# Scan of the second block: running sums loaded by DMA, and the per-head work put into another order

## The chip, the core and the metric

The kernel runs on one core of a Trainium2 chip. The time is the device time of the program in microseconds; the median of three runs counts. Five engines work from their own queues, in order: TensorE (PE, matrix products), VectorE (DVE), ScalarE (ACT, functions by table), GpSimd (POOL) and SyncE (SP), which here issues every DMA. They meet only in semaphore waits.

## The reference

Two transformer blocks on one sequence of 512 positions with 1024 channels, all in float32. The change touches only the scan in the mixer of the second block:

```python
a_cum = jnp.cumsum(log_a, axis=-1)
seg = a_cum[..., :, None] - a_cum[..., None, :]
decay_in = jnp.exp(jnp.where(causal, seg, -jnp.inf))
cb = jnp.einsum("bclgn,bcsgn->bcgls", cc, bc)
y_diag = jnp.einsum("bcgjls,bcsgjp->bclgjp", cb[:, :, :, None] * decay_in, x_)
decay_to_end = jnp.exp(a_cum[..., -1:] - a_cum)
states = jnp.einsum("bclgn,bcgjl,bclgjp->bcgjpn", bc, decay_to_end, x_)
...
y_off = jnp.einsum("bclgn,bcgjpn,bcgjl->bclgjp", cc, prev, jnp.exp(a_cum))
```

There are 32 heads in 4 groups of 8, and 4 chunks of 128 positions. `log_a` is `dt * a`, a number for each position and head; `a_cum` is its running sum inside a chunk.

## The kernel before

**Weights.** All weight products are cut into 361 units of 8 blocks. A block is one 128x128 piece of a weight times 128x512 of the input, in three matmuls (L755, L757, L759), since each float32 operand is split into a high part and a remainder. For each unit SP loads 512 KB into one of three raw buffers (L1892), ACT rounds it to the high part (L1128, a "cut") and DVE subtracts (L1420, the second half of the cut). The cut is ticked three units before its use.

**Order.** `score()` writes one list of ticks by hand. Each engine walks through the whole list and issues what it has for each tick, so the list sets the order on every engine. `woven(main, side, every, lead)` lets `lead` blocks of the main work pass and then puts one step of the side work behind every `every` blocks. In `seg(g)` (g = 1 to 4) the main work is 64 to 112 blocks and the side work is `ssd(g - 1)`, the scan of one group. Segment 1 runs `ya_main` beside group 0; segments 2, 3 and 4 begin with `zgroup(g - 2)`, four tiles z of 8 blocks each. The ticks of two finished z tiles are held and released together, behind blocks 16 and 32. A z tile costs ACT a silu (L1263), DVE a product (L1580), ACT a square (L1145) and, for the second and third of a group, POOL an addition (L1842). There is one buffer for the silu, so the steps of two tiles follow one another across ACT and DVE.

**The scan of a group.** `xrow` (four times) turns x on PE (L1030) and DVE scales it by dt into XD (L1739). `bturn` turns B (PE L1038, ACT L1370). `cb` is C times B (PE L1046), masked by DVE (L1746). `state` c = 0, 1, 2: POOL scales XD[c] by the decay to the chunk's end into the one buffer `stmp` (L1866), PE multiplies (L1054), DVE carries the sum on (L1752; L1756 and L1758). `decay` of a head: PE spreads the head's row of running sums to all 128 partitions by a product of a column of `pairR` with `acR`, the sums in high part and remainder (L1063); ACT makes `exp` of three chunks into EX (L1378), the differences by four Relu (L1381) and their `exp` into SGM (L1384); DVE multiplies SGM by CB (L1764) and POOL multiplies EX by C (L1872). SGM and EX have six buffers for eight heads, so heads 6 and 7 wait for the output of heads 0 and 1. `output` j: PE makes the result of heads 2j and 2j + 1 (L1073, L1079), which needs their SGM and EX and all three states; DVE adds the skip term (L1770).

**Tables.** ACT's Exp and Silu lie in different function tables; between them stands an ACT_TABLE_LOAD.

Below, "turn" always means one of the four xrow steps, and block k of a segment is counted from the segment's start; the first turn of each group stands behind block 6.

## Time and profile before

| | us |
|---|---|
| runs | 2361.22, 2362.50, 2362.77 |
| median | 2362.5 |
| profiled execution, its own time | 2362.4 |
| span of its profile | 2360.6 |
| PE busy (share of the span) | 2302.7 (98%) |
| DVE, ACT, POOL busy | 1168.1, 870.8, 155.1 |
| group 0 of the scan, first turn to about the last output | 1433 to 1475 |
| groups 1, 2 and 3 | 1529 to 1577, 1612 to 1660, 1695 to 1742 |

The span is what the profile's clock covers; the execution's own time is 1.8 us more. The stretches are times from the span's start. PE is the engine that sets the end, so the question for any work on another engine is whether PE waits for it.

### The profile page before, as it was taken

Reading aid. Unit: us, or ns where it says so; the run is one execution under the profiler, and the core shown is the slowest. Engines: PE = TensorE matmul, PEld = TensorE weight load, DVE = VectorE, ACT = ScalarE, POOL = GpSimd, SP = SyncE. Lnnn points to the kernel's source line nnn. Section 1 sums busy time; section 2 is a strip of 40 time slices with the busy share of each in tenths; the row PEclk is TensorE's granted clock in tenths of the full one; section 3 lists DMA queues with packets and bytes.
Section 4 is the critical chain, followed back from the end, with each engine's and each line's share of the span. In section 5 each row is a group of like instructions: output and inputs, shape, how many; then the busy total and the mean of one; then the engine's idle time right before and its main releaser. Section 6 shows DMA issues by size and latency. Waiting matters only on the chain.

```text
span 2360.6 us, 27446 instructions
## 1 busy us (share of the span) xinstructions
PE 2302.7 (98%) x11216; PEld 1842.1 (78%) x11216; DVE 1168.1 (49%) x1615; ACT 870.8 (37%) x1413; POOL 155.1 (7%) x145
## 2 busy tenths in 40 slices
PE   8999999999999999999999999999999999999998
PEld 6767788888777677888887877866778887888886
DVE  3765665543465744333335455556743345553453
ACT  3554322132354533322323236356363223332332
POOL 1111000000100010000010002022020001000001
PEclk9999999999999999999999999999999999999999
DMA  9323465522212122222232222211223222233222
GB/s 318 134 99 111 175 216 202 207 98 98 81 63 72 46 71 83 96 98 98 90 107 81 98 90 98 98 55 63 72 90 107 98 81 98 87 101 106 92 88 81
DMA packets 77518, 250.69 MB, mean 106 GB/s; under 512 B 8272, under 2 KB 16720, under 8 KB 77392
## 3 DMA queue, kind: packets, MB, share of 16 engines
q1 hardware_dynamic: 77392, 248.93, 30.4%
q8 instruction: 89, 1.46, 0.3%
q14 instruction: 37, 0.30, 0.0%
HBM read 244.70 MB, written 4.19 MB: 105 GB/s over the span
## 4 chain that ended last, share of the span: by engine, by line
PE 82%; ACT 3%; DVE 3%; issue 1%; POOL 1%; POOLq 0%; DVEq 0%; ACTq 0%
PE pb L755 25%; PE pb L759 24%; PE pb L757 24%; PE pb L979 1%; PE pb L1004 1%; PE pb L989 1%; PE pb L1073 1%; DVE slab L1684 1%; PE pb L779 1%; PE pb L775 1%; PE pb L777 1%; PE pb L1054 1%; PE pb L800 0%; PE pb L861 0%; ACT slab L1381 0%
## 5 line engine op out<-in xcount | busy, mean ns | idle before, releaser
L755 PE MATMUL pb<-hhi,whi 128*128 128x512 f32 x1976 | 787.0, 398 | 4.2 <-ACT hhi L1156 2.4
L1420 DVE TENSOR_TENSOR wlo<-raw,whi 128x1024 fp32r<-128x1024 f32 x361 | 449.1, 1248 | 686.9 <-ACT whi L1128 686.9
L757 PE MATMUL pb<-hhi,wlo 128*128 128x512 f32 x1976 | 771.3, 390 | 1.7 <-DVE wlo L1420 1.7
L759 PE MATMUL pb<-hlo,whi 128*128 128x512 f32 x1976 | 771.4, 390 | 0.4 <-DVE hlo L1416 0.4
L1128 ACT ACTIVATE whi<-raw 128x1024 fp32r<-128x1024 f32 x361 | 379.2, 1056 | 688.8 <-PE pb L759 672.0
L755 PEld LDWEIGHTS pb<-hhi,whi 128*128 128x128 f32 x1976 | 371.2, 188 | 98.5 <-issue 24.5
L759 PEld LDWEIGHTS pb<-hlo,whi 128*128 128x128 f32 x1976 | 371.2, 188 | 81.8 <-DVE hlo L1416 1.6
L757 PEld LDWEIGHTS pb<-hhi,wlo 128*128 128x128 f32 x1976 | 371.7, 188 | 78.8 <-DVE wlo L1420 2.7
L755 PE MATMUL pb<-ahi,whi 128*128 128x512 f32 x848 | 336.2, 396 | 1.4 <-ACT ahi L1310 0.7
L759 PE MATMUL pb<-alo,whi 128*128 128x512 f32 x848 | 331.3, 391 | 0.0
L757 PE MATMUL pb<-ahi,wlo 128*128 128x512 f32 x848 | 331.2, 391 | 0.0
L755 PEld LDWEIGHTS pb<-ahi,whi 128*128 128x128 f32 x848 | 159.9, 189 | 39.2 <-issue 6.1
L759 PEld LDWEIGHTS pb<-alo,whi 128*128 128x128 f32 x848 | 159.7, 188 | 34.5 <-DVE alo L1416 0.8
L757 PEld LDWEIGHTS pb<-ahi,wlo 128*128 128x128 f32 x848 | 159.9, 189 | 32.7 <-issue 0.7
L1842 POOL TENSOR_TENSOR slab<-slab 128x512 f32<-128x512 f32 x44 | 62.0, 1410 | 1588.2 <-ACT slab L1145 1587.3
L1511 DVE SCALAR_TENSOR_TENSOR slab<-slab,vec 128x509 f32<-128x509 f32 (+2 forms) x132 | 99.0, 750 | 4.7
L1416 DVE TENSOR_TENSOR alo<-slab,ahi 128x512 fp32r<-128x512 f32 x90 | 62.3, 692 | 67.9 <-ACT ahi L1227 50.4
L1431 DVE SCALAR_TENSOR_TENSOR slab<-slab,small 128x1024 f32<-128x1024 f32 x70 | 89.9, 1284 | 1.9
L1145 ACT ACTIVATE slab<-X 128x512 f32<-128x512 f32 x48 | 30.3, 632 | 109.3 <-PE pb L759 39.5
L1684 DVE TENSOR_TENSOR_SCAN slab<-slab,cst 128x128 f32<-128x128 f32 (+3 forms) x64 | 52.5, 820 | 31.0 <-ACT slab L1323 31.0
L1542 DVE TENSOR_TENSOR slab<-slab,pb 128x512 f32<-128x512 f32 x66 | 45.0, 682 | 43.6 <-PE pb L759 43.6
L1227 ACT ACTIVATE ahi<-slab 128x512 fp32r<-128x512 f32 x66 | 41.7, 632 | 66.0 <-DVE slab L1542 65.8
(232 smaller groups left out, 1702.9 us busy)
## 6 DMA issues: line engine op xcount, KB each, us to landing
raw<-stream SPq DMA_DIRECT2D x361, 512.0 KB, 3.3
slab<-ada_w SPq DMA_DIRECT2D x80, 512.0 KB, 5.0
early<-ada_w SPq DMA_DIRECT2D x32, 256.0 KB, 7.6
X<-xT SPq DMA_DIRECT2D x8, 256.0 KB, 4.5
ya<-slab SPq DMA_DIRECT2D x8, 256.0 KB, 2.3
slab<-ya SPq DMA_DIRECT2D x8, 256.0 KB, 4.9
outT<-X SPq DMA_DIRECT2D x8, 256.0 KB, 2.1
cst<-consts SPq DMA_DIRECT2D x1, 576.0 KB, 7.2
```

The source lines that it names most:

```text
L755: e.matmul(out, wh, hi, start=s.k == 0, stop=False)
L757: e.matmul(out, wl, hi, start=False, stop=False)
L759: i = e.matmul(out, wh, lo, start=False, stop=s.last)
L1128: e.activation(whi[:, u % NW, :], raw[:, u % NRAW, :], ACT.Copy).then_inc(*a_cut.up(u))
L1227: e.activation(a_out[f % HALF][0], SG[f % 6], ACT.Copy).then_inc(*a_half.up(("f", l, f)))
L1416: e.tensor_tensor(out, src, hi.bitcast(F), ALU.subtract).then_inc(*v_half.up(key))
L1420: e.tensor_tensor(wlo[:, u % NW, :], raw[:, u % NRAW, :], whi[:, u % NW, :].bitcast(F), ALU.subtract).then_inc(*v_cut.up(u))
L1431: e.scalar_tensor_tensor(o, a, cond[:, k:k + 1], o, ALU.mult, ALU.add).then_inc(*v_mod.up(("fma", n)))
L1511: e.scalar_tensor_tensor(t[:, d:], u[:, :S - d], W(name, (width - 1 - d) * tiles + i), t[:, d:], ALU.mult, ALU.add).then_inc(*v_conv.up((k ...
L1542: e.tensor_tensor(t, t, b, ALU.mult).then_inc(*v_ev.up(tile))
L1684: e.tensor_tensor_scan(p[:, 0:wd][:, ::-1], RS[n % 4][:, 0:wd][:, ::-1], C("late", S - wd)[:, 0:wd][:, ::-1], 1.0, ALU.mult, ALU.max).then ...
L1842: e.tensor_tensor(acc, acc, sq_of(sid, d), ALU.add).then_inc(*p_sum.up((sid, d)))
```

## The change

- `decay` has no PE part any more. DVE's sums `dtac` are written to DRAM once (`sums_dram`, 32 heads by 512 positions), and SP loads the row of each head into EX on all 128 partitions, in head order, two heads ahead of the decay that reads it; the load of head n waits for the output of head n - 6. `acR`, `pairR`, and the ACT and DVE steps that filled them are gone.
- ACT's part of `decay` reads EX (in SBUF) instead of the PSUM bank, first the four Relu, then the `exp` of three chunks in place, then the other.
- DVE's and POOL's part of `decay` is now a tick of its own, `masked`.
- `ssd` has another order: decays 0 and 1 stand between the turns, decay 2 at bturn, and so on; one step behind every 2 blocks for all groups (before: 2 for group 0, 1.2 for the others), but 17 steps instead of 25.
- POOL scales XD[0] and XD[1] at their turns into two buffers `STMP`, and XD[2] at the tick of state 0.

```diff
-SSD_FIRST, SSD_NEXT = 2, 1.2
+SSD_EVERY = 2
...
     def ssd(g):
         for c in range(4):
             tick("xrow", g, c)
+            if c % 2 == 0:
+                tick("decay", g, c // 2)
             yield 1
         tick("bturn", g)
+        tick("decay", g, 2)
         yield 1
         tick("cb", g)
+        tick("masked", g, 0)
         yield 1
-        for c in range(3):
-            tick("state", g, c)
-            yield 1
-        for j in range(4 + SKEW):
-            if j < 4:
-                for hh in (2 * j, 2 * j + 1):
-                    tick("decay", g, hh)
-                    yield 1
-            if j >= SKEW:
-                tick("output", g, j - SKEW)
-                yield 2
+        tick("state", g, 0)
+        tick("decay", g, 3)
+        tick("masked", g, 1)
+        yield 1
+        tick("state", g, 1)
+        tick("masked", g, 2)
+        yield 1
+        tick("state", g, 2)
+        tick("decay", g, 4)
+        tick("masked", g, 3)
+        yield 1
+        tick("decay", g, 5)
+        for j in range(4):
+            tick("output", g, j)
+            if j < 2:
+                tick("decay", g, 6 + j)
+                tick("masked", g, 4 + j)
+            if j in (1, 2):
+                tick("masked", g, 5 + j)
+            yield 2
...
-            e.matmul(b, pairR[:, H:H + 1].to_broadcast([64, P]), acR[:, :], start=True, stop=True).then_inc(*t_ssd.up(("decay", g, h)))
...
-            e.activation(ex[:, P:], b[:, P:], ACT.Exp).then_inc(*a_ssd.up(("ex", g, h)))
-                m = e.activation(sg[:, quarter(c)], b[:, quarter(c)], ACT.Relu, bias=nat[:, o:o + 1], scale=-1.0)
+                m = e.activation(sg[:, quarter(c)], ex[:, quarter(c)], ACT.Relu, bias=nat[:, o:o + 1], scale=-1.0)
             m.then_inc(*a_ssd.up(("fall", g, h)))
             w.wait_ge(a_ssd, ("fall", g, h))
+            e.activation(ex[:, P:], ex[:, P:], ACT.Exp).then_inc(*a_ssd.up(("ex", g, h)))
...
+        def scaled_rows(g, c):
...
+            if c == 2:
+                w.wait_ge(t_ssd, ("state", g, 0))
             elif g:
+                w.wait_ge(t_ssd, ("state", g - 1, 2))
...
+        def fall():
+
+            n = falls[0]
+            if n < 32:
+                falls[0] += 1
+                if n >= 6:
+                    w.wait_ge(t_ssd, ("y", *divmod(n - 6, 8)))
+                e.dma_start(EX[n % 6], sums_dram[n:n + 1, :].to_broadcast([P, S])).then_inc(*d_ac[n % 6].up(n))
```

Where the steps now stand. **ACT, group 1, from its last cut ahead of the group.** L1263 and L1145 are silu and square of the z tiles, L1370 is the turned B. Before, the two z tiles stand ahead of all heads:

```order
L1370 ACTIVATE spare_67<-pb 128x512
L1263 ACTIVATE slab<-pb 128x512
L1145 ACTIVATE slab<-slab 128x512
L1263 ACTIVATE slab<-pb 128x512
L1145 ACTIVATE slab<-slab 128x512
L1128 ACTIVATE whi<-raw 128x1024
L1378 ACT_TABLE_LOAD
L1378 ACTIVATE slab<-pb 128x384
L1381 ACTIVATE slab<-pb,slab 128x128 x4
L1384 ACTIVATE slab<-slab 128x512
```

Now (L1373 is the turned B; L1383, L1386, L1387 are the Relu and the two exp of a head; L1268 and L1150 silu and square):

```order
L1387 ACTIVATE slab<-slab 128x512
L1133 ACTIVATE whi<-raw 128x1024
L1383 ACTIVATE spare_68<-spare_71,slab 128x128 x4
L1386 ACTIVATE spare_71<-spare_71 128x384
L1387 ACTIVATE spare_68<-spare_68 128x512
L1373 ACTIVATE spare_66<-pb 128x512
L1383 ACTIVATE spare_69<-spare_72,slab 128x128 x4
L1386 ACTIVATE spare_72<-spare_72 128x384
L1387 ACTIVATE spare_69<-spare_69 128x512
L1268 ACT_TABLE_LOAD
L1268 ACTIVATE slab<-pb 128x512
L1150 ACTIVATE slab<-slab 128x512
```

Three heads have moved ahead of the z tiles, and what stands behind the tiles begins with a cut and a table load again; ACT_TABLE_LOAD stands 28 times in the program, before 22.

**DVE, group 1, from the turns to the third head.** L1739 is XD, L1746 CB, L1752, L1756 and L1758 the states, L1580 the product of a z tile, L1764 the product with CB. Before:

```order
L1739 TENSOR_TENSOR slab<-pb,slab 128x512 x2
L1746 TENSOR_TENSOR slab<-pb,cst 128x512
L1752 COPY slab<-pb 128x512
L1756 TENSOR_TENSOR slab<-slab 128x512
L1758 TENSOR_TENSOR slab<-slab,pb 128x512
L1756 TENSOR_TENSOR slab<-slab 128x512
L1758 TENSOR_TENSOR slab<-slab,pb 128x512
L1580 TENSOR_TENSOR slab<-slab 128x512 x2
L1420 TENSOR_TENSOR wlo<-raw,whi 128x1024
L1764 TENSOR_TENSOR slab<-slab 128x512
```

Now (L1583 is the z product, L1423 the cut):

```order
L1739 TENSOR_TENSOR slab<-pb,slab 128x512 x3
L1583 TENSOR_TENSOR slab<-slab 128x512 x2
L1423 TENSOR_TENSOR wlo<-raw,whi 128x1024
L1746 TENSOR_TENSOR slab<-pb,cst 128x512
L1764 TENSOR_TENSOR slab<-slab 128x512
L1752 COPY slab<-pb 128x512
L1764 TENSOR_TENSOR spare_68<-spare_68,slab 128x512
L1756 TENSOR_TENSOR slab<-slab 128x512
L1758 TENSOR_TENSOR slab<-slab,pb 128x512
L1764 TENSOR_TENSOR spare_69<-spare_69,slab 128x512
```

The z products and the cut have moved ahead of CB and of every state, and products of heads stand between the states.

**POOL, group 1.** L1866 scales XD, L1842 is the addition for the z tiles, L1872 (now L1880) the product of a head. Before:

```order
L1866 TENSOR_TENSOR spare_68<-slab 128x512 x3
L1842 TENSOR_TENSOR slab<-slab 128x512
L1872 TENSOR_TENSOR slab<-slab 128x384
L1872 TENSOR_TENSOR spare_72<-spare_72,slab 128x384
L1872 TENSOR_TENSOR spare_73<-spare_73,slab 128x384
```

Now:

```order
L1866 TENSOR_TENSOR spare_67<-slab 128x512
L1866 TENSOR_TENSOR stmp_60<-slab 128x512
L1842 TENSOR_TENSOR slab<-slab 128x512
L1880 TENSOR_TENSOR slab<-slab 128x384
L1866 TENSOR_TENSOR spare_67<-slab 128x512
L1880 TENSOR_TENSOR spare_71<-spare_71,slab 128x384
L1880 TENSOR_TENSOR spare_72<-spare_72,slab 128x384
```

The third scaling has moved behind the addition and behind a head's product.

**DVE, group 1, at the last outputs.** L1770 is the skip term of an output. Now the last head's product stands behind two z products and a cut:

```order
L1770 SCALAR_TENSOR_TENSOR slab<-slab,vec,pb 128x512
L1764 TENSOR_TENSOR slab<-slab 128x512 x2
L1583 TENSOR_TENSOR slab<-slab 128x512 x2
L1423 TENSOR_TENSOR wlo<-raw,whi 128x1024
L1770 SCALAR_TENSOR_TENSOR slab<-slab,vec,pb 128x512
L1764 TENSOR_TENSOR spare_68<-spare_68,slab 128x512
L1770 SCALAR_TENSOR_TENSOR slab<-slab,vec,pb 128x512
```

Before, it stood ahead of them:

```order
L1764 TENSOR_TENSOR slab<-slab 128x512
L1764 TENSOR_TENSOR spare_69<-spare_69,slab 128x512
L1770 SCALAR_TENSOR_TENSOR slab<-slab,vec,pb 128x512 x2
L1580 TENSOR_TENSOR slab<-slab 128x512 x2
L1420 TENSOR_TENSOR wlo<-raw,whi 128x1024
L1770 SCALAR_TENSOR_TENSOR slab<-slab,vec,pb 128x512
```

## Rows read from the trace of the kernel before

**Rows 1.** PE waits in the four groups, microseconds 1400 to 1800: total, times, longest.

```profile
PE pb L1054 <- POOL spare L1866: 5.4, 7, 1.1
PE pb L1073 <- DVE spare L1764: 3.8, 2, 1.9
PE pb L1073 <- DVE slab L1764: 2.1, 2, 1.9
```

**Rows 2.** Timeline of PE around one head's spreading product: start, duration, engine, line.

```profile
1452.01 0.40 PE L759 MATMUL pb<-alo,whi 128*128 128x512 f32 x1
1452.33 0.49 PE L1063 MATMUL pb<-acR,pairR 64*128 64x512 f32 x1
...
1453.09 0.40 PE L757 MATMUL pb<-ahi,wlo 128*128 128x512 f32 x1
1453.33 0.39 PE L759 MATMUL pb<-alo,whi 128*128 128x512 f32 x1
```

**Rows 3.** Windows of groups 1 and 2: length, busy (count) PE, PEld, DVE, ACT, POOL, clock, DMA.

```profile
1529.40:1577.00 47.60, 43.94 (x259) 30.66 (x257) 24.87 (x31) 29.38 (x65) 15.61 (x13) 0.96 0.14 45
1612.20:1660.00 47.80, 44.19 (x260) 31.17 (x258) 25.93 (x33) 29.64 (x65) 15.61 (x13) 0.96 0.15 52
```

**Rows 4.** Timeline of PE, group 0: first turn, states 0 and 1.

```profile
1433.34 0.60 PE L1030 MATMUL pb<-cst,slab 128*128 128x128 f32 x4
...
1444.75 1.02 PE L1054 MATMUL pb<-spare,spare 128*128 128x512 f32 x2
...
1447.11 1.10 PE L1054 MATMUL pb<-spare,spare 128*128 128x512 f32 x2
```

**Rows 5.** Timeline of PE, group 1: first turn, last state, outputs.

```profile
1529.41 0.60 PE L1030 MATMUL pb<-cst,slab 128*128 128x128 f32 x4
...
1542.59 1.10 PE L1054 MATMUL pb<-spare,spare 128*128 128x512 f32 x2 [1.08 <-POOL spare L1866]
...
1555.67 0.29 PE L1073 MATMUL pb<-slab 128*64 128x128 f32 x1 [1.95 <-DVE spare L1764]
...
1563.11 0.66 PE L1073 MATMUL pb<-spare,slab 128*64 128x128 f32 x8
...
1567.05 0.66 PE L1073 MATMUL pb<-slab 128*64 128x128 f32 x8
```

**Rows 6.** Timeline of ACT, group 1: cut, z tiles, cut, table, heads.

```profile
1529.66 1.04 ACT L1128 ACTIVATE whi<-raw 128x1024 fp32r<-128x1024 f32 x1
...
1545.78 0.63 ACT L1145 ACTIVATE slab<-slab 128x512 f32<-128x512 f32 x1 [10.12 <-DVE slab L1580]
...
1547.65 0.63 ACT L1145 ACTIVATE slab<-slab 128x512 f32<-128x512 f32 x1 [0.76 <-DVE slab L1580]
1548.19 1.04 ACT L1128 ACTIVATE whi<-raw 128x1024 fp32r<-128x1024 f32 x1
1549.25 1.28 ACT L1378 ACT_TABLE_LOAD   x1
...
1552.63 0.47 ACT L1378 ACTIVATE spare<-pb 128x384 f32<-128x384 f32 x1
```

**Rows 7.** Timeline of DVE, group 1: state 2's two steps, then a z product.

```profile
1543.73 0.69 DVE L1756 TENSOR_TENSOR slab<-slab 128x512 f32<-128x512 f32 x1 [1.46 <-PE pb L1054]
...
1545.06 0.68 DVE L1580 TENSOR_TENSOR slab<-slab 128x512 f32<-128x512 f32 x1
```

**Rows 8.** Timeline of POOL, group 1: third scaling, z addition.

```profile
1540.97 1.48 POOL L1866 TENSOR_TENSOR spare<-slab 128x512 f32<-128x512 f32 x1 [1.39 <-PE pb L1054]
1548.42 1.28 POOL L1842 TENSOR_TENSOR slab<-slab 128x512 f32<-128x512 f32 x1 [5.98 <-ACT slab L1145]
```

**Rows 9.** DMA issues: KB each, median us from issue to landing.

```profile
ya<-slab SPq DMA_DIRECT2D x8, 256.0 KB, 2.3
slab<-ya SPq DMA_DIRECT2D x8, 256.0 KB, 4.9
```

**Rows 10.** Timeline of ACT ahead of group 2: the last silu before it.

```profile
1613.43 0.72 ACT L1364 ACTIVATE slab<-slab,vec 128x512 f32<-128x512 f32 x1 [3.12 <-DVE slab L1511]
```

More of the change, by code:

```diff
@@ L478, in score @@
     for g in range(1, 5):
[L479 removed]
+        run(woven(seg(g), ssd(g - 1), SSD_EVERY, SSD_LEAD))
     run(woven(zgroup(3), gated(2), 8))
@@ L555, in program @@
     d_late = signal("d_late", 16)
+    d_ac = [signal(f"d_ac{i}", 16) for i in range(6)]
+    d_sums = signal("d_sums", 16)
     d_ya = [signal(f"d_ya{i}", 16) for i in range(KD)]
@@ L1053, in state @@
             w.wait_ge(p_ssd, ("st", g, c))
-            e.matmul(b, Bn[:, quarter(c)], stmp, start=True, stop=True).then_inc(*t_ssd.up(("state", g, c)))
+            e.matmul(b, Bn[:, quarter(c)], STMP[c % 2], start=True, stop=True).then_inc(*t_ssd.up(("state", g, c)))
             give(("state", g, c), v_ssd, ("state", g, c))
-        def decay(g, h):
-            H = 8 * g + h
-            b = take(("decay", g, h))
-            w.wait_ge(a_ssd, "achi")
-            w.wait_ge(v_ssd, "aclo")
-            w.wait_ge(v_ssd, "pair")
-            e.matmul(b, pairR[:, H:H + 1].to_broadcast([64, P]), acR[:, :], start=True, stop=True).then_inc(*t_ssd.up(("decay", g, h)))
-            give(("decay", g, h), a_ssd, ("fall", g, h))
         def output(g, j):
@@ L1087, in tensor @@
               "values": values, "start": start, "turn": turn, "gather": gather, "dtturn": dtturn, "xrow": xrow, "bturn": bturn,
-              "cb": cb, "state": state, "decay": decay, "output": output}
+              "cb": cb, "state": state, "output": output}
         for name, *a in ticks:
@@ L1911, in evac, with dtturn @@
                 e.dma_start(ya_dram[i], SPILL[i % 4]).then_inc(*d_ya[i].up("out"))
+        def dtturn():
+            w.wait_ge(v_ssd, ("scan", 3))
+            e.dma_start(sums_dram, dtac[0:32, :]).then_inc(*d_sums.up("out"))
+            w.wait_ge(d_sums, "out")
+            for _ in range(2):
+                fall()
+        falls = [0]
+        def fall():
[5 more added lines that the diff above has]
+                e.dma_start(EX[n % 6], sums_dram[n:n + 1, :].to_broadcast([P, S])).then_inc(*d_ac[n % 6].up(n))
         def fetch(i):
@@ L1939, in sync @@
         fma(16)
-        do = {"cut": lambda u: load() if u > 2 else None, "fma": fma, "evac": evac, "fetch": fetch, "final": final}
+        do = {"cut": lambda u: load() if u > 2 else None, "fma": fma, "evac": evac, "dtturn": dtturn, "decay": lambda g, h: fall(), "fetch": fetch, "final": final}
         for name, *a in ticks:
```

39 lines of the change are left out of this document (17 added, 22 removed).

## The prediction

> **What bounds the kernel now.** The page's table comes first: TensorE is busy for 98% of the span, so the end moves only by what TensorE no longer has to do or no longer waits for. The second view is the list of waits between microseconds 1400 and 1800, where the four groups of the scan lie [rows 1]: TensorE waits 5.4 us for GpSimd's scaled rows (L1866) ahead of the states, and 3.8 and 2.1 us for VectorE's products with CB (L1764) ahead of an output. The third is TensorE's timeline, which gives the price of one inserted step, and the windows of two groups for its clock. The fourth is the timelines of ScalarE, VectorE and GpSimd in group 1, because the new order has to be walked through on each of their queues.
>
> **The change part by part.**
>
> *The spreading products go.* From the L759 ahead of one to the second matmul behind it pass 1453.09 - 1452.01 = 1.08 us; two matmuls without it are 2 x 0.23 [rows 2]. One costs 0.62 us of TensorE's path, and 32 of them 19.8 us. Nothing hides it: this is the sure part.
>
> *The old waits.* They are 11.3 us [rows 1]. Behind the longest, the clock was granted at 0.96 of full speed in groups 1 and 2 [rows 3]: up to 0.04 x 47.6 = 1.9 us of work lost each, of which part fell into the idle time; I take 1.2 us each, 2.4 us. So the old order costs 19.8 + 11.3 + 2.4 = 33.5 us above a TensorE that never waits. The question is what the new order costs above the same line.
>
> *The grid of the new order.* It puts a step behind every second block, as group 0 had it. First turn to state 0 is 1444.75 - 1433.34 = 11.41 us, a state with two blocks about 2.27 us (1447.11 less 0.09 idle) [rows 4]. An output with three blocks takes 1567.05 - 1563.11 = 3.94 us [rows 5], with four 4.63. In group 1 the first turn is at 1529.41 [rows 5], so without waits state 0 stands at 1540.8, state 2 at 1545.4, output 0 at 1547.6 (its end at 1549.4), and output 3 at 1561.5.
>
> *ScalarE in group 1.* Its last cut begins at 1529.66, so head 0 begins at 1530.7. A table load takes 1.28 us; a head took 1552.63 - 1549.25 - 1.28 = 2.1 us from PSUM [rows 6]. Reading SBUF instead is not in the trace for this step; I bound it by 0 and 0.25 us (0.05 for each of five instructions, the spread between this engine's pitches) and take 2.13. Two z tiles cost a table load and two rounds of 1547.65 - 1545.78 = 1.87 us, 5.1 with the handovers, as long as VectorE answers at once; a cut takes 1.0 [rows 6]. In the new queue: head 0 to 1534.1, cut 1535.1, head 1 1537.2, turned B 1537.9, head 2 1540.0, z tiles 1545.1, cut 1546.2, head 3 with its table load 1549.5, head 4 1551.6.
>
> *VectorE.* The new queue has the z products and the cut ahead of CB and of the states. The cut waits for ScalarE's 1546.2 and ends at 1547.4. Then come CB, head 0, state 0, head 1, at 0.6 us each (two steps, of which one waits for the other, take 1545.06 - 1543.73 = 1.33 [rows 7]): head 1 is done at 1549.9. State 1, head 2 and state 2 end at 1553.2. Output 0 could start at 1547.6, and needs state 2 for its last quarter: it ends at 1553.7, 4.3 us late. So the wait for CB products doesn't go; it is handed on to a queue that now waits for the cut.
>
> *GpSimd.* The scalings 0 and 1 are early, and cost TensorE nothing any more. Scaling 2 stands behind the addition for the z tiles, which waits for ScalarE's second square at 1545.1. The addition takes 1.28 us, a head's product I bound by the same, the scaling took 1.48 [rows 8]: 1549.0 to 1549.2. State 2 is 3.7 us late, mostly inside the same delay, since output 0 waits for VectorE anyway; with half a microsecond of slower clock output 0 ends at 1554.2.
>
> *The loads.* 32 loads of 256 KB ride in SP's queue. Heads 0 to 5 of a group find theirs landed two heads ahead. Heads 6 and 7 can't: their buffer is free when output 0 ends. Landing is not in the trace for a repeated row; the bounds are 2.3 and 4.9 us of two other 256 KB transfers [rows 9], and I take 2.3, since nothing else is queued there. Behind the waiting SP stand the loads of the weight stream, issued three units (16 us) ahead of use, which a wait of 3 us doesn't exhaust. Behind the waiting ScalarE stand the z tiles and a cut. So head 6 starts at 1554.2 + 0.1 + 2.3 = 1556.6, heads 6 and 7 end at 1560.9, the z tiles at 1566.1, the cut at 1567.1, VectorE's half of it at 1568.4, the skip term of output 2 and the product of head 7 at 1569.7. Output 3 waits for this one: 1569.7 - 1561.5 = 8.2 us late in group 1.
>
> *Groups 2 and 3* begin with ScalarE later. The last silu ahead of group 2 is at 1613.43 [rows 10]; carried back by the distance of the groups (83.0 us) that is 1530.5 against about 1529.0, hence 1.4 us later all along, and 0.4 more where the cut behind block 24 now waits for a late TensorE. 10.0 us late each. *Group 0* has no z tiles: walked in the same way, ScalarE ends head 7 at about 1460 and output 3 is due at 1465. No wait, about 0.3 us of handovers.
>
> *Clock.* Each of the three groups gets a stall of over 3 us ahead of output 3. One such stall cost 1.2 us in two groups and nothing in the third; 0.8 each, 2.4 us, between 0 and 5.7 (three times the 1.9 above).
>
> *Table loads.* Six more on ScalarE. The order of groups 1 to 3 above contains them; where they hide nothing else changes. In the trace a load takes 1.28 us and the next instruction starts at once [rows 6]. The Trainium skill, "ScalarE: Activation LUTs", section "What ACT_TABLE_LOAD costs", gives 2.66 us a switch, with 1.38 of draining behind the load. By that the chains of three groups would each be some 4 us longer, and the kernel about 2371. This case's rows show no such drain, and they decide.
>
> *Nothing else.* ScalarE's and VectorE's one-time steps for the old operands go, under cover of TensorE's blocks; the write of the sums and its wait stand 30 us ahead of the first head.
>
> **The sum.** New order: 0.3 + 8.2 + 10.0 + 10.0 + 2.4 = 30.9 us, old order 33.5. The profiled execution took 2362.4 us, 0.1 below the median. 2362.5 - 2.6 is 2359.9; as VectorE's and ScalarE's steps in the walk are rounded up to their handovers, I take 0.5 us less: 2359.4. The products leave TensorE, and nearly all of it comes back as waits, because ScalarE is now the limit inside a group: 8 heads, 4 z tiles, 3 cuts and 4 table loads are 17 + 7.5 + 3 + 5.1 = 33 us of unbroken work between head 0 and the last cut, and the grid leaves 31 us for it.
>
> **The rivals.**
> - *Full gain.* The heads begin early enough that TensorE never waits. For it speaks that ScalarE idled 10.12 us at the z tiles before [rows 6], which the new order lets it use. Against it stand the 33 us. It would give 2362.5 - 33.5 + 0.3 = 2329.
> - *ScalarE's work alone.* If the buffers of heads 6 and 7 were filled without delay behind output 0, output 3 would be 1.9 us less late in group 1, and 2.3 in the others; about 2353.
> - *Late loads, slower than before.* A row of DRAM read 128 times lands late. ScalarE waits for it at head 6, in front of the z tiles and the cut, and TensorE pays each microsecond three times. At 4.9 us [rows 9] it is 3 x 2.6 = 7.8 us more: 2367. With the clock at its upper bound 2370. It decides from a landing of 3.4 us for slower at all, 5 us (or 4 with the clock) for slower than can be told.
>
> **How the numbers follow.** Forecast 0.54, full gain 0.10, ScalarE alone 0.14, late loads 0.22. About 0.2% (4.7 us) is what a measurement can tell from no change. The forecast's own range is 2355 to 2364 (heads at 2.1 or 2.35 us, clock 0 to 5.7); of its 0.54, 0.18 is faster than 2357.8 and 0.36 inside. Late loads are 0.18 slower and 0.04 inside. Faster 0.42, same 0.40, slower 0.18. The range leaves out the full gain and part of the rest: 2350 to 2369.
>
> **What would show it.** Right: no L1063, 32 loads into EX; TensorE waits at output 3 of groups 1 to 3 for L1764, 3 to 5 us each, at state 2 for L1866, 3 to 4 us, and not at all in group 0; ScalarE without idle time from head 0 on except at head 6. Wrong: a TensorE without these waits (the full gain), or loads that land in over 3.4 us. My walk through the queues would be wrong if VectorE came to CB before the cut was ready.

## The result, and the profile after

The changed kernel takes 2378.3 us (median of 6 runs, 2375.5 to 2379.8); the kernel before, on the same chip, 2361.5 us (median of 6). The ratio is 1.0071, with a 95% interval of 1.0060 to 1.0082: slower, by about 17 us. The forecast was 2359.4 with a range to 2369.0, so the time lies outside it and on the other side. The profiled execution took 2376.0 us, with a span of 2373.9 us (2360.6 before).

The list of PE's waits in the four groups, microseconds 1430 to 1790 (what is waited for: us in total, times, longest), answers to [rows 1]. L1068 is the state's matmul, L1078 and L1084 are an output's, L1866 is GpSimd's scaling, L1764 VectorE's product with CB:

```profile
PE pb L1068 <- POOL spare L1866: 17.3, 3, 6.2
PE pb L1078 <- DVE spare L1764: 11.2, 2, 5.7
PE pb L1078 <- DVE slab L1764: 7.4, 2, 5.5
PE pb L771 <- DVE wlo L1423: 1.4, 2, 0.7
PE pb L1084 <- DVE slab L1758: 1.1, 1, 1.1
```

The 11.3 us of before have become 37.0 (the L771 row, a wait for a cut, is left out: before has 1.7 us of the same). They stand where the prediction put them: state 2 and output 3 of groups 1 to 3. PE's timeline of group 1 shows both, and what follows the first one (L769, L771 and L773 are the three matmuls of a block):

```profile
1547.23 2.04 PE L1068 MATMUL pb<-spare,spare 128*128 128x512 f32 x2 [4.84 <-POOL spare L1866]
1548.29 1.42 PE L769 MATMUL pb<-hhi,whi 128*128 128x512 f32 x1
1549.50 0.63 PE L771 MATMUL pb<-hhi,wlo 128*128 128x512 f32 x1
1549.93 0.63 PE L773 MATMUL pb<-hlo,whi 128*128 128x512 f32 x1
...
1550.65 0.40 PE L771 MATMUL pb<-hhi,wlo 128*128 128x512 f32 x1
1550.88 0.40 PE L773 MATMUL pb<-hlo,whi 128*128 128x512 f32 x1
...
1571.05 0.44 PE L1078 MATMUL pb<-slab 128*64 128x128 f32 x1 [5.73 <-DVE spare L1764]
```

The state's matmul takes 2.04 us where it took 1.02 [rows 4], and the next products follow one another at 0.43 us, then at 0.23. The windows say why (columns as in [rows 3]; the clock is third from the end):

```profile
1526.00:1573.00 47.00, 36.43 (x230) 27.97 (x230) 25.84 (x30) 33.69 (x67) 17.36 (x13) 0.91 0.31 101
1612.00:1660.00 48.00, 36.29 (x223) 27.71 (x223) 27.93 (x33) 33.82 (x67) 17.10 (x13) 0.89 0.32 107
...
1571.00:1574.00 3.00, 2.96 (x28) 2.88 (x28) 0.00 (x0) 0.00 (x0) 0.00 (x0) 0.50 0.44 164
```

The granted clock of the two groups is 0.91 and 0.89, against 0.96 before, and behind output 3 it is 0.50: TensorE works at 1.2 GHz instead of 2.4, after 5.7 us without work.

In some executions of every kernel, before too, the scan begins some 5 us earlier than in others (first turn of group 0 at 1428.5 instead of 1433.3), since TensorE's clock stays up at places far ahead of it; so intervals inside the scan are compared first, and medians second.

**An account that every run below uses.** Take the interval from group 1's first turn to group 2's. Subtract TensorE's idle time (the bracketed waits of its timeline, without those of 0.2 us), then the work lost to the lower clock (over windows of 1 us, busy time times one less the granted clock), then what the kernel adds to TensorE's queue: 8 spreading products, or filler. The rest should be the same in all kernels. It is read from one profiled execution of each.

| kernel | interval | idle | lower clock | products or filler | rest |
|---|---|---|---|---|---|
| before | 82.95 | 4.4 | 1.7 | 5.0 | 71.9 |
| after | 86.35 | 11.3 | 3.2 | 0 | 71.9 |
| d1 new order, products | 87.56 | 8.4 | 3.4 | 4.4 | 71.4 |
| d2 old order, loads | 84.83 | 10.5 | 2.3 | 0 | 72.0 |
| d3 no late loads | 82.28 | 8.7 | 1.4 | 0 | 72.2 |
| d4 third buffer | 86.68 | 9.1 | 5.8 | 0 | 71.8 |
| e5 slower pace | 77.52 | 4.5 | 2.3 | 0 | 70.7 |
| e8 filler | 85.06 | 2.1 | 0 | 11.2 | 71.8 |
| f4 filler, state 2 only | 86.32 | 8.6 | 1.4 | 4.3 | 72.0 |
| h1 head 5 early | 73.32 | 1.8 | 0 | 0 | 71.5 |
| h2 the same, products | 76.66 | 0.7 | 0 | 4.4 | 71.6 |

The rests lie between 70.7 and 72.2 us. Over all four groups the changed kernel idles 25.8 us more than before (2.7, 6.9, 8.1 and 8.1), loses 12.1 us instead of 3.3 to the lower clock (6.1 behind state 2 and 6.1 behind output 3), and saves 19.8 us of products: 14.8 us slower. Measured from the first turn of group 0 to the last group norm's spreading product are 12.5 us (-3.0, +3.4, +5.3 and +6.9 in the four groups). Another 0.9 us comes behind it, where the changed kernel's execution lost 1.6 us to the lower clock and that of before none.

Three more views. GpSimd in group 1: the addition, a head's product and the scaling that state 2 waits for:

```profile
1542.43 1.27 POOL L1842 TENSOR_TENSOR slab<-slab 128x512 f32<-128x512 f32 x1 [7.35 <-ACT slab L1150]
1543.66 1.98 POOL L1880 TENSOR_TENSOR slab<-slab 128x384 f32<-128x384 f32 x1
1545.60 1.49 POOL L1866 TENSOR_TENSOR spare<-slab 128x512 f32<-128x512 f32 x1
```

ScalarE in group 1: a table load and what follows it; head 6, which waits for its load:

```profile
1537.13 1.28 ACT L1268 ACT_TABLE_LOAD   x1
1538.42 0.60 ACT L1268 ACTIVATE slab<-pb 128x512 f32<-128x512 f32 x1
...
1556.91 1.28 ACT L1383 ACTIVATE slab<-slab 128x128 f32<-128x128 f32 x4 [2.28 <-DMA slab<-sums]
```

And the DMA issues (KB each, median us from issue to landing), which answer to [rows 9]:

```profile
raw<-stream SPq DMA_DIRECT2D x361, 512.0 KB, 3.4
slab<-sums SPq DMA_DIRECT2D x17, 256.0 KB, 3.7
spare<-sums SPq DMA_DIRECT2D x15, 256.0 KB, 3.8
```

### The profile page after: what moved, and what is told of

It is laid out like the page before. It is cut to its first block, busy times and chain, and to the rows that moved or that the text cites. A ratio compares the mean times of both kernels' runs of the same rounds, so it can differ in the third digit from the quotient of the medians.

```text
span 2373.9 us, 27414 instructions
## 1 busy us (share of the span) xinstructions
PE 2291.4 (97%) x11184; PEld 1846.1 (78%) x11184; DVE 1176.3 (50%) x1613; ACT 883.9 (37%) x1418; POOL 158.4 (7%) x145
## 4 chain that ended last, share of the span: by engine, by line
PE 78%; DVE 5%; ACT 4%; issue 2%; DMA 1%; POOL 0%; DVEq 0%; POOLq 0%; SPq 0%; ACTq 0%
PE pb L769 24%; PE pb L773 23%; PE pb L771 23%; DVE slab L1514 1%; PE pb L993 1%; PE pb L1018 1%; DVE wlo L1423 1%; PE pb L1003 1%; ACT whi L1133 1%; ACT slab L1383 1%; DVE slab L1687 1%; PE pb L793 1%; PE pb L789 1%; PE pb L791 1%; PE pb L814 0%
## 5 line engine op out<-in xcount | busy, mean ns | idle before, releaser
L1423 DVE TENSOR_TENSOR wlo<-raw,whi 128x1024 fp32r<-128x1024 f32 x361 | 448.3, 1246 | 708.8 <-ACT whi L1133 708.8
L769 PE MATMUL pb<-hhi,whi 128*128 128x512 f32 x1976 | 786.8, 398 | 3.4 <-ACT hhi L1161 2.2
L771 PE MATMUL pb<-hhi,wlo 128*128 128x512 f32 x1976 | 772.1, 391 | 1.4 <-DVE wlo L1423 1.4
L773 PE MATMUL pb<-hlo,whi 128*128 128x512 f32 x1976 | 772.4, 391 | 0.4 <-DVE hlo L1419 0.4
L769 PEld LDWEIGHTS pb<-hhi,whi 128*128 128x128 f32 x1976 | 372.3, 188 | 94.8 <-issue 20.1
L773 PEld LDWEIGHTS pb<-hlo,whi 128*128 128x128 f32 x1976 | 371.8, 188 | 82.3 <-DVE hlo L1419 1.6
L771 PEld LDWEIGHTS pb<-hhi,wlo 128*128 128x128 f32 x1976 | 372.3, 188 | 80.4 <-issue 3.2
L769 PE MATMUL pb<-ahi,whi 128*128 128x512 f32 x848 | 335.5, 396 | 1.4 <-ACT ahi L1315 0.7
L773 PE MATMUL pb<-alo,whi 128*128 128x512 f32 x848 | 331.0, 390 | 0.0
L771 PE MATMUL pb<-ahi,wlo 128*128 128x512 f32 x848 | 331.0, 390 | 0.0
L769 PEld LDWEIGHTS pb<-ahi,whi 128*128 128x128 f32 x848 | 159.9, 189 | 37.3 <-issue 4.2
L773 PEld LDWEIGHTS pb<-alo,whi 128*128 128x128 f32 x848 | 159.7, 188 | 34.2 <-DVE alo L1419 0.7
L771 PEld LDWEIGHTS pb<-ahi,wlo 128*128 128x128 f32 x848 | 160.1, 189 | 33.1 <-issue 0.7
L1842 POOL TENSOR_TENSOR slab<-slab 128x512 f32<-128x512 f32 x44 | 61.8, 1405 | 1596.8 <-ACT slab L1150 1595.9
L1150 ACT ACTIVATE slab<-X 128x512 f32<-128x512 f32 x48 | 30.3, 632 | 109.2 <-PE pb L773 39.5
```

The lines of the kernel that those rows point to most:

```text
L769: e.matmul(out, wh, hi, start=s.k == 0, stop=False)
L771: e.matmul(out, wl, hi, start=False, stop=False)
L773: i = e.matmul(out, wh, lo, start=False, stop=s.last)
L1423: e.tensor_tensor(wlo[:, u % NW, :], raw[:, u % NRAW, :], whi[:, u % NW, :].bitcast(F), ALU.subtract).then_inc(*v_cut.up(u))
L1842: e.tensor_tensor(acc, acc, sq_of(sid, d), ALU.add).then_inc(*p_sum.up((sid, d)))
```

## The experiments

Each median stands beside that of the kernel before from the same chip.

**1. Order alone, loads alone.** The first kernel is the changed one with the old products on TensorE; the second is the old order with the loads.

```diff
 d1, against after
-    e.dma_start(EX[n % 6], sums_dram[n:n + 1, :].to_broadcast([P, S]))
+    e.matmul(b, pairR[:, H:H + 1].to_broadcast([64, P]), acR[:, :], ...)
 d2, against before
-    e.matmul(b, pairR[:, H:H + 1].to_broadcast([64, P]), acR[:, :], ...)
+    e.dma_start(EX[n % 6], sums_dram[n:n + 1, :].to_broadcast([P, S]))
```

> The kernel before with only the new order of the scan (heads between the turns, the products with CB ticked on their own, two buffers for the scaled rows); the running sums still come from the spreading product on TensorE. The order theory: what makes the changed kernel slow is the order, since the z tiles now stand ahead of CB, of the states and of the third scaling, and ahead of head 7's product. Then the waits at state 2 and output 3 of groups 1 to 3 are here too. The 32 products (0.62 us each) come back, but 24 of them fall into those waits, and the landing time ahead of head 6 (2.3 us of idle ScalarE) goes: about 2378, between 2374 and 2381. The load theory: the slow part is the loads (landing 3.7 us, SyncE held up to 8 us in front of the weight loads, 8 MB more traffic); without them the new order is as good as it looks, and the time is 2366 or less.

> The changed kernel with the old order of the scan (all heads behind the states, steps 2 and 1.2 blocks apart, one buffer for the scaled rows, filled at each state), but with the running sums loaded. The order theory: the products leave TensorE (19.8 us less work), and the old waits grow, because head 1 is bound by ScalarE's queue and TensorE now arrives at output 0 some 3.7 us earlier in groups 1 to 3; group 0 gains 5 us whole, the others 1 to 2 us each. The landing for heads 6 and 7 is hidden, since ScalarE reaches head 6 only 6 us behind output 0. About 2353, between 2349 and 2357. The load theory: the loads cost what they cost in the changed kernel, so 2370 or more.

Measured: 2378.5 us for the order alone (ratio 1.0084, 1.0062 to 1.0105) and 2366.5 us for the loads alone (1.0032, 1.0018 to 1.0046), beside 2360.9. The order alone is as slow as the whole change. Its waits are the same two, shorter:

```profile
PE pb L1066 <- POOL spare L1878: 10.4, 3, 3.5
PE pb L1085 <- DVE spare L1776: 8.4, 2, 4.2
PE pb L1085 <- DVE slab L1776: 4.4, 2, 4.2
```

So the new order costs some 18 us by itself, and taking 32 products off TensorE under that order brings nothing. With the old order the loads are no gain either: there TensorE waits 6.4 us at output 0 of groups 1 to 3 (three of the six waits in these two rows):

```profile
PE pb L1067 <- DVE spare L1753: 15.8, 4, 6.4
PE pb L1067 <- DVE slab L1753: 7.8, 2, 6.4
```

The loads-alone time lies between what the two theories said; neither had both costs.

**2. No loads for heads 6 and 7.** These two heads of each group take what lies in their buffers, so this part of the computation is left out.

```diff
+    if n % 8 >= 6:
+        return
     if n >= 6:
         w.wait_ge(t_ssd, ("y", *divmod(n - 6, 8)))
     e.dma_start(EX[n % 6], ...)
```

> The changed kernel without the loads of heads 6 and 7 of each group (8 of 32; these heads compute on what is left in their buffers), everything else in place. It measures what the landing behind output 0 costs. The order theory: ScalarE's idle 2.3 us ahead of head 6 goes in groups 1 to 3, and output 3 comes that much earlier; the waits at state 2 stay: about 2371.5, between 2369 and 2374. The load theory (late landing and held SyncE carry the loss): at or below 2364.

Measured: 2363.7 us (ratio 1.0020, 1.0008 to 1.0033), 14.6 below the changed kernel; the spans differ by 12.7. The waits:

```profile
PE pb L1068 <- POOL spare L1867: 17.2, 3, 6.2
PE pb L1078 <- DVE spare L1765: 6.7, 2, 3.5
PE pb L1078 <- DVE slab L1765: 3.5, 1, 3.5
```

State 2 is as it was; output 3 waits 3.2 to 3.5 us instead of 5.5 to 5.7, which is 6.5 us less in groups 1 to 3, and not at all in group 0. That is 8.5 us of idle time, and the lower clock takes 8.6 us instead of 12.1. The late loads are real, and they cost about twice what the prediction gave them; the number is the load theory's, although the order's cost stands beside it.

**3. A third buffer for the scaled rows**, so that GpSimd does all three ahead of the z tiles.

```diff
-    STMP = [slot(40), stmp1[:, :]]
+    STMP = [slot(40), stmp1[:, :], C("late")]
-    if c < 2:
+    if c < 3:
         scaled_rows(g, c)
```

> The changed kernel with a third buffer for the scaled rows, so that GpSimd scales XD[2] at its turn and no longer behind the z addition and head 0's product. The order theory: the waits of TensorE at state 2 (4.8, 6.2, 6.2 us) vanish, but output 0 is bound by VectorE's states, which stand behind the z products and the cut; what is gained is the slower clock behind the wait and some contention between GpSimd and VectorE, 1.5 to 2.5 us a group: about 2372, between 2370 and 2375. If the wait for GpSimd were the cause by itself, 17 us would go: about 2361. The load theory: no change, 2378.

Measured: 2372.2 us (1.0054, 1.0036 to 1.0072). That is what the order theory gave. The interval overlaps that of the changed kernel (1.0060 to 1.0082), so the waits say more than the time. The state is on time, and the stall stands one step further on, as walked through in the prediction. In group 1:

```profile
1542.50 0.29 PE L1078 MATMUL pb<-slab 128*64 128x128 f32 x1 [3.08 <-DVE spare L1764]
...
1547.36 0.47 PE L1084 MATMUL pb<-slab 128*64 128x128 f32 x1 [1.70 <-DVE slab L1758]
```

3.08 + 1.70 us replace 4.84 at state 2. SyncE issues head 6's load, which waits for output 0, 27.0 us behind the first turn, as before the edit (26.8): output 0 has come no earlier.

**4. What makes the loads land late.** The same 32 loads from 128 different rows of other data; the running sums are thereby left out.

```diff
-    e.dma_start(EX[n % 6], sums_dram[n:n + 1, :].to_broadcast([P, S]))
+    e.dma_start(EX[n % 6], io["xT"][0:P, :])
```

> The changed kernel, with the 32 loads of a repeated row replaced by 32 loads of 256 KB of other data that lie in DRAM as 128 different rows, so the running sums are left out of the result. Repeated-row theory (the 3.7 us from issue to landing come of reading one row 128 times): they land in 2.3 to 2.6 us, output 3 waits 1 us less in each group, and the time is 2370 to 2375. Queue theory (any 256 KB behind the stream of the weights and next to it land in 3.7 us): landing 3.5 us or more and 2376 to 2380.

Measured: 2375.3 us (4 runs, 2370.2 to 2378.7), too wide to decide, but the landings decide:

```profile
slab<-xT SPq DMA_DIRECT2D x17, 256.0 KB, 3.5
spare<-xT SPq DMA_DIRECT2D x15, 256.0 KB, 3.6
```

That one row is read 128 times costs 0.2 us of the 3.7. The rest is what a read of this size takes at this place of the kernel; the weight stream's 512 KB take 3.4.

**5. What the lower clock costs.** Matmuls of no use in front of the stalls, first at both places, then at state 2 alone.

```diff
+    if g: tick("warm", 6)             # 5 in the second kernel
     tick("state", g, 2)
 ...
+    if g and j == 3: tick("warm", 7)  # not in the second kernel
     tick("output", g, j)
```

> The changed kernel, with 6 matmuls of no use (about 0.62 us each) ahead of state 2 and 7 ahead of output 3 in groups 1 to 3, so that TensorE works through 3.7 and 4.3 us of stalls of 4.8 to 6.2 us. Clock theory (the lower clock behind a stall costs its 12.1 us of lost work in full, on top of the stall): the granted clock stays at 1.0 in these groups, and the time is 2366 to 2371. Cover theory (the work lost behind state 2 falls into the wait for output 3, and only what is lost behind output 3 counts, about half): 2370 to 2375. If the lower clock costs nothing, because ScalarE's chain sets the pace anyway: 2376 to 2380.

> The changed kernel with 5 matmuls of no use ahead of state 2 alone, in groups 1 to 3; the filler of the run before took 0.86 us a piece, so this is 4.3 us in stalls of 4.8 to 6.2 us. Full-price theory (what the lower clock loses behind state 2, about 2 us a group, is added to the time): 2371 to 2374. Cover theory (it falls into the wait for output 3, which grows by the same when the clock is kept): 2376 to 2380, and the wait for output 3 rises by 1.5 us or more a group.

The first expectation priced a matmul of the filler at 0.62 us; it took 0.86, so the fillers were 5.2 and 6.0 us long and swallowed the whole stall in group 1. Measured: 2370.7 us (1.0042, 1.0027 to 1.0058) with both, 2376.0 us (1.0062, 1.0049 to 1.0076) at state 2 alone, beside 2378.3 without. With both, the clock stays up in groups 1 to 3 (1.00 in the windows of groups 1 and 2), and 7.6 us are gained by doing more work. The profiled executions show 4.4 us of them in groups 1 to 3 (1.3, 1.0 and 2.1). At state 2 alone the intervals of groups 1 and 2 stay what they were: 86.32 and 88.12 us, against 86.35 and 88.23. Its waits in groups 1 to 3:

```profile
PE pb L1080 <- DVE spare L1766: 11.9, 2, 5.9
PE pb L1080 <- DVE slab L1766: 6.2, 1, 6.2
PE pb L1086 <- DVE slab L1760: 4.6, 3, 1.5
```

TensorE arrives earlier at output 0 and waits 1.5 us there, and output 3 comes no earlier. ScalarE's head 6 in group 1 shows the same: its cut is on time, it waits for the load all the longer, and it starts 30.6 us behind the first turn in both kernels:

```profile
1557.47 1.28 ACT L1385 ACTIVATE slab<-slab 128x128 f32<-128x128 f32 x4 [3.93 <-DMA slab<-sums]
```

So the cover theory holds for state 2: work lost there falls into a wait that comes anyway. Behind output 3 no further wait of the group follows, and what is lost is lost. The whole 12.1 us of lost work are therefore no price. The 6.1 us lost behind output 3 are one; the filler's gain, 7.6 us by the medians and 4.4 in the traces, lies on both sides of that number.

**6. Pace.** Steps behind every third block instead of every second, in groups 0 to 2; then also in the last group, over the z tiles' blocks.

```diff
-    run(woven(seg(g), ssd(g - 1), SSD_EVERY, SSD_LEAD))
+    run(woven(seg(g), ssd(g - 1), 3 if g < 4 else SSD_EVERY, SSD_LEAD))
 e6 on top of it
+    def last():
+        yield from seg(4)
+        yield from woven(zgroup(3), gated(2), 8)
-    run(woven(zgroup(3), gated(2), 8))
+    run(woven(last(), ssd(3), 2.6, SSD_LEAD))
```

> The changed kernel with one number changed: in the first three of the four groups of the scan a step stands behind every third block of the main product instead of every second. Nothing is added or taken away. The trace of the changed kernel puts 3.0, 10.6 and 11.7 us of TensorE's waits, and 0, 3.2 and 4.2 us of work at the lower clock, between the first turns of groups 0, 1, 2 and 3, together 32.7 us. Pace theory (ScalarE's 33 us of unbroken work stand against 31 us of blocks, while some 40 us of the same group are left without steps): nearly all of it goes, 2342 to 2352, and TensorE waits at state 2 and output 3 only in the last group. Chain theory (the waits hang on landings, on handovers and on the z tiles and move with the steps): the waits come back behind the later outputs, and the time stays at 2368 or more.

> As the kernel with the slower pace, and the last group's steps too are spread, one behind every 2.6 blocks, over the 32 blocks that they have now and the 32 of the z tiles behind them. Pace theory: the last group's 11.7 us of waits and 4.7 us of lower clock go as well, less what the z tiles now wait for outputs 0 to 3: 2328 to 2340. Rival: the z tiles' products hold PSUM until the outputs are out, and the waits of the last group turn into waits for banks: no better than the kernel before it, 2345 or more.

Measured: 2355.2 us (0.9974, 0.9963 to 0.9984) and 2348.7 us (0.9956, 0.9936 to 0.9976), beside 2362.5: both faster than before, and both above what the pace theory gave them. State 2 waits no more in the groups so paced, and one stall a group is left. Group 1's interval falls from 86.35 to 77.52 us. VectorE ahead of the stall that is left (a convolution, a cut, the skip term of output 1, and only then the products with CB), and the output 2 that waits for it:

```profile
1556.08 2.32 DVE L1514 SCALAR_TENSOR_TENSOR slab<-slab,vec 128x511 f32<-128x511 f32 x3
1558.32 1.22 DVE L1423 TENSOR_TENSOR wlo<-raw,whi 128x1024 fp32r<-128x1024 f32 x1
1559.45 0.15 DVE L1460 TENSOR_SCALAR small<-pb 128x4 f32<-128x4 f32 x1
1559.53 0.74 DVE L1770 SCALAR_TENSOR_TENSOR slab<-slab,vec,pb 128x512 f32<-128x512 f32 x1
1560.18 2.09 DVE L1764 TENSOR_TENSOR slab<-slab 128x512 f32<-128x512 f32 x2
```

```profile
1561.01 1.12 PE L1078 MATMUL pb<-slab 128*64 128x128 f32 x8 [4.49 <-DVE slab L1764]
```

**7. Pace is not all: place.** The old order at a slower pace, without and with the loads; and the paced new order with three products moved between the outputs.

```diff
 f2 (before) and f3 (old order, loads)
-    SSD_FIRST if g == 1 else SSD_NEXT
+    (SSD_FIRST, 1.8, 1.8, SSD_NEXT)[g - 1]
 f1, against e6
     tick("output", g, j)
 ...
-        tick("masked", g, 4 + j)
-    if j in (1, 2):
+    if j == 0:
+        tick("masked", g, 4)
+    yield 1
+    if j < 3:
         tick("masked", g, 5 + j)
-    yield 2
+    yield 1
```

> The kernel before with one number changed: in groups 1 and 2 a step stands behind every 1.8 blocks instead of every 1.2; the spreading products stay on TensorE. Pace theory: of the 4.4 and 4.3 us of waits and 3.3 us of lower clock in these groups 7 to 10 us go, 2350 to 2356. Rival (the kernel before waits on fixed distances between queues, the 1.1 us behind a scaled row and the 1.9 us at output 1, whatever the pace): 2359 to 2363.

> The kernel with the old order of steps and the loads instead of the products, with a step behind every 1.8 blocks instead of every 1.2 in groups 1 and 2. At 1.2 it waited 10.5 and 10.0 us in them and lost 2.3 and 2.6 us to the lower clock. Pace theory: most of it goes, and the products' own 20 us show at last: 2341 to 2350. Rival (heads 6 and 7 wait for their late loads at any pace): 2358 or more.

> The kernel with all four groups at the slower pace, with the products with CB of heads 5, 6 and 7 (and GpSimd's beside them) moved from the step of an output to half way between two outputs. In the kernel it starts from, one stall per group is left: output 2 waits 4.5, 4.7 and 6.2 us for the product of head 5, which stands on VectorE behind the convolution of an x tile and the skip term of output 1. Pace theory: the stalls go, with 2.2, 2.2 and 2.8 us of work at the lower clock behind them, together 22.6 us: 2324 to 2334. Rival: the product moved ahead waits for ScalarE's head 5 and holds the convolution and VectorE's half of the cut, and the stall is only handed on: 2343 to 2350.

Measured: 2374.4 us (1.0055, 1.0041 to 1.0069), 2377.7 us (1.0067, 1.0051 to 1.0083) and 2359.3 us (0.9988, 0.9979 to 0.9997), beside 2362.9. All three missed their pace theory, by 18 us and more, and not for the reasons that the rivals gave. In the old order the slower pace carries GpSimd's first scaling behind the addition for the z tiles, and state 0 waits 6 us. GpSimd, then PE, of the first kernel:

```profile
1544.12 1.26 POOL L1842 TENSOR_TENSOR slab<-slab 128x512 f32<-128x512 f32 x1 [67.84 <-ACT slab L1145]
1545.35 2.02 POOL L1866 TENSOR_TENSOR spare<-slab 128x512 f32<-128x512 f32 x1
```

```profile
1547.51 2.05 PE L1054 MATMUL pb<-spare,spare 128*128 128x512 f32 x2 [6.02 <-POOL spare L1866]
```

In the second, TensorE waits 6.0 us there too, and another 6.6 and 6.3 us at the sum of the group norm (L845), which needs GpSimd's addition behind the z tiles.

In the third, the stall at output 2 is gone, and the product of head 7, moved by one block too many, stands behind the four steps of the group norm: output 3 waits 10.3 us (two of the three waits of this row).

```profile
PE pb L1085 <- DVE spare L1771: 26.1, 3, 10.3
```

So a slower pace helps only where no step slides behind a long one of the main product.

**8. One product moved.** Of the three, only that of head 5, to stand behind head 4's at output 0; and the same with the old products instead of the loads.

```diff
 h1, against e6
-    tick("masked", g, 4 + j)
+    if j == 0:
+        tick("masked", g, 4)
+        tick("masked", g, 5)
 h2, against h1: as d1 stands to after
```

> The kernel with all four groups at the slower pace, with one product moved: VectorE's product with CB for head 5 stands behind that of head 4, at output 0, and not behind the skip term of output 1. Those of heads 6 and 7 stay where they were. Place theory (a stall hangs on what stands ahead of a product in VectorE's queue, here the convolution of an x tile): the stalls of 4.5 and 4.7 us in groups 1 and 2 go, with 2.2 us of lower clock behind each, 1 us comes back at the group norm's spreading product, the last group's 6.2 us go in part: 2328 to 2338. Rival (ScalarE's late heads 6 and 7 take over, as in the kernel with three products moved): 2345 or more.

> The same order and pace as the kernel with head 5's product moved, but with the old spreading products on TensorE and no loads. If the pace is what the new order lacked and the loads are worth what TensorE no longer does: 32 times 0.62 us more than that kernel, 18 to 22 us. If the late loads still eat part of it, less: 8 to 16 us more. If the new order is no good at this pace either, both kernels stand above 2355.

Measured: 2338.9 us (0.9905, 0.9888 to 0.9922) and 2344.7 us (0.9931, 0.9917 to 0.9945), beside 2361.6. The first ends 0.9 us above what the place theory gave it. Its longest waits in all four groups:

```profile
PE pb L1085 <- DVE slab L1771: 5.5, 1, 5.5
PE pb L882 <- POOL small L1835: 2.4, 2, 1.3
PE pb L1091 <- DVE slab L1765: 2.0, 2, 1.4
```

In group 0 neither kernel has idle time or a lower clock, so 94.24 - 89.85 = 4.39 us is the pure price of eight products: 0.55 us each, 17.7 us for 32. Yet the kernels differ by 5.8 us only, less than any expectation. The loads' kernel idles 5.5 us at output 3 of the last group and loses 2.9 us to the clock behind it.

**9. The late loads at this pace.** Left out again; then kept, over seven buffers, with which head 6's load no longer waits for output 0.

```diff
 h4, against h1 (h3: the lines of d3)
-    EX = [slot(i) for i in (36, 37, 38, 44, 45, 46)]
+    EX = [slot(i) for i in (36, 37, 38, 44, 45, 46)] + [C("late")]
-    if n >= 6:
-        w.wait_ge(t_ssd, ("y", *divmod(n - 6, 8)))
+    if n >= 7:
+        w.wait_ge(t_ssd, ("y", *divmod(n - 7, 8)))
```

> The kernel with the slower pace and head 5's product moved, without the loads of heads 6 and 7 and ScalarE's waits for them (these two heads then take what lies in their buffers; part of the computation is left out). In the kernel it starts from, ScalarE waits 4.2 us at head 6 of the last group and TensorE 5.5 us at its output 3, with 2.9 us at the lower clock behind. Late-load theory (what is left of the loads' 18 us sits there): 2328 to 2333. Rival (the z tiles ahead of head 7 hold it anyway): 2336 or more.

> The same start, and nothing left out: the loads go around over seven buffers instead of six (the seventh is a row of constants that the scan doesn't read), so head 6's load waits for the last output of the group before and is there in time; head 7's still waits for output 0, but has ScalarE's head 6 and z tiles to land behind. Late-load theory: as without these loads, 2328 to 2334. Rival: 2336 or more.

Measured: 2335.2 us (0.9890, 0.9874 to 0.9906) and 2334.7 us (0.9888, 0.9869 to 0.9907), beside 2361.8. Both end a little above what was expected (2333 and 2334) and below the rival. Their intervals overlap that of the kernel they start from (0.9888 to 0.9922), so the trace has to carry the reading. With seven buffers the longest wait of the last group falls from 5.5 to 2.5 us, and its clock stays up:

```profile
PE pb L1085 <- DVE slab L1771: 2.5, 1, 2.5
```

Without the loads the wait is 2.2 us, and 1.7 us are lost to the clock behind it. So one more buffer takes away nearly all that the late loads still cost. The loads now bring 10.0 of their 17.7 us (h2 less h4); most of the rest is idle time that this kernel has and h2 has not (9.5 us against 2.9). The last kernel, with nothing of the computation left out, is 27 us faster than the kernel before, and some 44 us faster than the changed one was.

## Why the prediction was wrong

It put the new order at 30.9 us above a TensorE that never waits, and the old one at 33.5. By the account, the new one is at 49.1 (37.0 idle, 12.1 lower clock) and the old one at 34.4. The step that failed is the walk to output 3, with the landing and the stretched steps in it, and the clock term behind it.

- **How late output 3 is: the largest miss.** The walk had it 40.3 us behind the first turn of group 1, 8.2 us late, and 10.0 us late in groups 2 and 3. It started at 44.7, 46.2 and 46.4 us; the grid without waits has 32.1, so it was 12.6, 14.1 and 14.3 us late. Of the 4.4 us by which the walk was short in group 1, 2.0 had gathered when output 0 let head 6's load go (26.8 us behind the first turn, the walk had 24.8), the landing adds 1.4, and 1.0 comes behind head 6.
- **Group 0: walked as free of waits, 0.3 us.** It idled 3.0 us: 1.1 at output 0 for VectorE's state, and 1.9 at output 3, since ScalarE waited 2.7 and 0.8 us for the loads of heads 6 and 7.
- **Place and cause of the stalls: right.** State 2 waits for the scaling and output 3 for the product of head 7, in groups 1 to 3. VectorE came to CB behind the cut (1544.71, which is 18.4 us behind the first turn; the walk had 18.0). The third buffer moved the stall and did not remove it.
- **The products: nearly right.** 0.62 us each from [rows 2] was the price in the old order; in the new one they cost 0.55.
- **The clock term: too small.** "One such stall cost 1.2 us in two groups and nothing in the third; 0.8 each" took the loss behind a 1.9 us wait for that behind two waits of about 5 us a group. The lost work was 12.1 us; behind the stall ahead of output 3, which the term was for, it was 6.1 instead of 2.4, above the bound of 5.7 too. The old loss was itself put too low: 1.7 us in each of groups 1 and 2 by the account, not 1.2. What is lost behind state 2 was covered.
- **Landing: the wrong row.** The term "I take 2.3, since nothing else is queued there" was taken from a write to DRAM [rows 9]. The loads are reads, and landed in 3.7 us. The other row of that group was a read (4.9), and so is the weight stream. That is 1.4 us in each of three groups. By the prediction's own rule (slower from 3.4 us on) this alone made the sign doubtful. ScalarE's idle time ahead of head 6 was still only 2.3, 1.6 and 2.0 us, since it came to head 6 late itself.
- **Late loads as a whole.** They were given 6.4 us (the distance to the rival of ScalarE alone); without them the kernel is 14.6 us faster by the medians and 12.7 by the spans. In groups 1 to 3 the waits at output 3 fall by 6.5 us, which is what the rival had. What it left out is group 0's output 3 (1.9 us) and 3.5 us of lower clock; together these are 11.9.
- **Work side by side.** Each step was priced by a row in which its neighbour rested. The head's product on GpSimd took 1.98 us instead of 1.28, and state 2 was 4.8 to 6.2 us late, not 3.7. VectorE's state steps, which output 0 needs, took 1.48 us instead of 0.69. That neither the lower clock nor the third scaling set the end of output 0 in group 1 is shown by the filler and the third buffer (head 6's load went at 26.8 and 27.0 us); how much of the 2.0 us is VectorE's two longer steps was not measured by itself.
- **Waiting behind a waiting TensorE.** ScalarE's cut at 1551.32 waited 2.32 us for products that state 2's stall had delayed. It was foreseen for groups 2 and 3 with 0.4 us. In this kernel it cost nothing further: with filler at state 2 the cut waits 0.7 us, and head 6 starts no earlier, because its load is still on its way.
- **SP held: longer, and free as foreseen.** It waited up to 8.0 us for an output, not 3. TensorE waited for no weight that it had not waited for before.
- **Table loads: right.** The row above shows the next step 1.29 us behind the start of a load. The Trainium skill, "ScalarE: Activation LUTs", section "What ACT_TABLE_LOAD costs", adds a drain of 1.38 us; this trace has none, and the slower time has other causes.
- **The rivals.** "Late loads" had the right sign and the right mechanism with too small a factor: TensorE pays in all four groups, and the clock on top. That the order alone could cost 18 us was no rival at all. The prediction saw 33 us of ScalarE's work against 31 us of cover and took that as given. Its own listing of the order says otherwise: in groups 1 and 2 the steps use 38 of 80 blocks (17 turns of 2, and a lead of 4), and 42 stand empty.

The expected gain did not go to one place. The new order at its pace takes 18 us, the loads give 18 and take back 13 to 15. At a pace that fits, with one product moved and one buffer more, the same change is worth 27 us.

What stays open: 2.3 us of the 14.8 that the account gives are not found in the four intervals, and the filler's 7.6 us by the medians stand against 4.4 in the traced groups. The two traces differ in group 0 too, where neither has filler: in one the clock fell behind a wait of 2.2 us, in the other it stayed up behind 1.9.

## What to carry to other kernels

Before taking work off the busiest engine, ask whether the queues that feed it fit the pace of the steps: 33 us of work against 31 us of cover means that whatever leaves TensorE comes back as waiting. Price a transfer by a row that goes the same way (a read by a read), a step beside a busy neighbour by a row in which the neighbour is busy, and a long stall with the lower clock behind it unless another wait follows. Where an order is spread by a number, look at each queue for what now stands ahead of each step: 1.8 for 1.2 cost 12 us, and one product moved gained 10.

## What the runs showed of the hardware

- TensorE at 1.2 GHz: around waits of 4.5 us and more in the scan the granted clock was 0.50 for some microseconds every time, mostly with 1.4 to 4.1 us of work lost. Between 1.9 and 3.6 us it fell behind some waits and not behind others: before, it fell behind 1.95 and 1.90 us and not behind 1.92. With filler in both stalls it stayed at 1.00, although the filler's results went nowhere; groups 1 and 2 of that kernel:

```profile
1526.75:1611.80 85.05, 82.75 (x437) 62.27 (x436) 53.60 (x68) 47.16 (x87) 18.55 (x14) 1.00 0.24 83
1611.80:1699.00 87.20, 82.92 (x437) 62.22 (x436) 54.72 (x70) 47.49 (x87) 18.54 (x14) 1.00 0.26 84
```

- VectorE and GpSimd slow one another. GpSimd's head product took 1.98 us beside VectorE's cut, and 1.01 us alone in the kernel before. VectorE's step L1756 in group 1 begins inside three products of GpSimd, and takes 1.48 us, against 0.69 in [rows 7]:

```profile
1547.05 4.27 POOL L1880 TENSOR_TENSOR spare<-spare,slab 128x384 f32<-128x384 f32 x3
```

```profile
1547.56 1.48 DVE L1756 TENSOR_TENSOR slab<-slab 128x512 f32<-128x512 f32 x1
1549.08 0.69 DVE L1758 TENSOR_TENSOR slab<-slab,pb 128x512 f32<-128x512 f32 x1
```

  The step with one operand in PSUM, right behind it, takes 0.69 in the same company. The Trainium skill, "SBUF — State Buffer", section "Who interferes with whom", says that a VectorE instruction with two SBUF inputs contends with a GpSimd instruction that reads SBUF, and one with a single such input doesn't; the rows agree.
- A DRAM row repeated to 128 partitions lands in 3.7 to 3.8 us, 128 different rows in 3.5 to 3.6.
